# Hybrid RWKV-7 / Mamba-2 / short-convolution layer: two activation parts streamed side by side

## Chip, core and metric

The kernel runs on one core of a Trainium2 chip. The metric is device time in microseconds of that core for one execution, the median of three timed runs.

## What is computed

All data is fp32. One layer is applied to x of 256 tokens by 2048 channels:

```python
h = rmsnorm(x, norm_w[l])
p = h @ w_in[l]                                   # 2048 x 17552
pa, pb, pc, pg = jnp.split(p, ...)
oa = rwkv7_branch(pa, ...)                        # each 256 x 1024
ob = mamba2_branch(pb, ...)
oc = short_conv_branch(pc, sc_conv_w[l])
o = jnp.stack([oa, ob, oc], axis=2)
yb = jnp.einsum('btnw,nwd->btnd', o, w_branch[l]) # three products 1024 x 2048
gates = jax.nn.sigmoid(pg.reshape(bsz, seq, N_BRANCH, D_MODEL))
merged = jnp.sum(gates * yb, axis=2)
x = x + merged @ w_out[l]                         # 2048 x 2048
return rmsnorm(x, final_norm_w)
```

Nearly all the arithmetic is in the four dense products. The branches are a token shift and a delta-rule recurrence (RWKV-7, done in blocks of 32 tokens), a chunked state-space scan (Mamba-2) and a short convolution.

## The kernel before

**Split products.** A dense product is not done in plain fp32. Weight and activation are each split into a high part rounded to fp32r and a low part that is the rest; three fp32r matmuls add up in one accumulation: high weight by high activation, high weight by low activation, low weight by high activation. The weight tile (128 x 128) is the stationary operand, the activation (128 channels x 256 tokens) streams. `hhi` and `hlo` hold the parts of h, later of `merged`; `ohi` and `olo` those of a branch's output.

**Chunks and strips.** Weights arrive in chunks of 512 rows by 256 columns (`raw`, four slots). ScalarE rounds a chunk to `whi` (`split_hi`), VectorE subtracts to get `wlo` (`split_lo`), and TensorE takes it in two halves t = 0, 1 of 128 columns, four triples each (`half_chunk`, `triple`). Both splits run two chunks ahead of TensorE (`AHEAD`). Four chunks make a strip of two finished tiles, 256 columns of 2048 rows. A tile lies in columns 0 to 255 of a PSUM bank; strips use banks 0 and 1 or 2 and 3 in the order `BANKS = (0, 2, 0, 0, 2)`, so that the fourth strip of an iteration takes the banks of the third.

**Stages.** (1) 28 chunks: low-rank columns, B and C of Mamba-2 with their convolutions, the first r, k, v, g. (2) The branch loop, eight iterations j of 20 chunks (12 in the last), each for 128 channels. An iteration is written out by hand in 40 slots, one for each half chunk; at fixed slots every engine gets its piece of the branch work. For the prediction these matter: at slot 0 ScalarE exponentiates the decays and evicts the strip of v and g (`shift_pair`: a copy to `pq` and a scaled copy to `qq` of each tile); at 1 VectorE forms k, b and r with the decays; at 4 TensorE transposes them; at 5 ScalarE copies the transposes (`vt`, `kdbd`); at 5 and 7 VectorE masks the scores; at 8 ScalarE evicts x and z, at 9 to 12 VectorE does the conv taps and a triangular solve in 15 steps; at 16 the second, at 24 the third strip is evicted, at 32 the next r and k. TensorE's chain u, w, y and the states goes from slot 19 to 31. (3) The gates: for each of three branches, eight strips of four gate chunks (banks 2, 3) and two chunks of w_branch (y, banks 0, 1); ScalarE takes the sigmoid of the gate out of PSUM, VectorE multiplies by y out of PSUM and adds to `merged` (`gated`). The last iteration of the loop runs the first two gate strips. (4) The output stage, where `merged` is stationary and w_out streams in 256 columns: L1432 to L1434, 768 matmuls. (5) The tail: row sums, root, scaling, store.

**Order.** Each engine runs its list in the order written and waits on semaphores. `tile_done` and `chunk_used` tell of a finished tile; `tile_out` counts evicted tiles, and TensorE waits for it before it takes a bank again; `lo_done` counts split chunks. `gy_ok` counts the products with y.

## Time and profile before

| | |
|---|---|
| three runs | 1282.39 us median (1281.48 to 1282.54) |
| span of the profiled execution | 1279.8 us |
| busy | TensorE 97%, weight load 92%, VectorE 64%, ScalarE 46%, GpSimd 5% |
| granted TensorE clock | 0.997 of full speed, mean |
| chain that ended last | TensorE 81%, VectorE 9%, issue 4%, ScalarE 3% |
| DMA | 194.91 MB, 152 GB/s |

The profiled execution is one run, 0.2% under the median of the timed ones. Busy time is the time in which an engine has an instruction in flight. Matmuls overlap in the pipe (each is 283 ns long), so their sum is more than the span, and what one costs is seen from the distance between the starts of two. The chain that ended last is followed back from the end, at each step to what released it.

### The profile page before, as it was taken

What the parts mean: (1) busy time and instruction counts of PE and PEld (TensorE: products, weight loads), DVE (VectorE), ACT (ScalarE), POOL (GpSimd) and SP (SyncE); (2) the same over time, 40 slices, a digit from 0 to 9 for tenths busy, and PEclk for the clock granted to TensorE, in tenths of its full rate; (3) what the DMA queues carried; (4) which work ended last, traced back from release to release, by engine and by line L of the source; (5) the groups of instructions that cost most, each with busy time, mean ns of one, the idle gap of its engine ahead of it and who ended that gap; (6) DMA issues with size and microseconds to landing.
All of it is one profiled execution on the core that took longest, in us unless ns stands there. A gap on an engine that the chain in (4) does not pass through costs nothing.

```text
span 1279.8 us, 27520 instructions
## 1 busy us (share of the span) xinstructions
PE 1244.8 (97%) x10118; PEld 1175.6 (92%) x10118; DVE 822.3 (64%) x1340; ACT 589.2 (46%) x893; POOL 62.5 (5%) x93
## 2 busy tenths in 40 slices
PE   6999999999999999999999999999999999999996
PEld 5998889899898998998989989999999999999996
DVE  4787759578486695784867956654555455555653
ACT  5555346255354462643534535444444444335443
POOL 2001000010010000100001003000000000000000
PEclk9999999999999999999999999999999999999998
DMA  5774544445345344553544445465555666557652
GB/s 163 193 198 117 138 114 123 127 121 155 105 131 135 103 128 120 141 146 95 145 118 115 104 146 175 156 197 181 182 178 171 191 190 188 181 179 250 211 183 96
DMA packets 298623, 194.91 MB, mean 152 GB/s; under 512 B 23799, under 2 KB 297424, under 8 KB 297936
## 3 DMA queue, kind: packets, MB, share of 16 engines
q1 hardware_dynamic: 298308, 193.72, 51.8%
q8 instruction: 30, 0.49, 0.2%
q10 hardware_dynamic: 268, 0.56, 0.1%
q14 instruction: 17, 0.14, 0.0%
HBM read 191.61 MB, written 2.10 MB: 151 GB/s over the span
## 4 chain that ended last, share of the span: by engine, by line
PE 81%; DVE 9%; issue 4%; ACT 3%; DMA 1%; DVEq 0%; SPq 0%; ACTq 0%
PE ps L1153 21%; PE ps L1154 20%; PE ps L1155 20%; DVE lots L888 3%; PE ps L1434 2%; PE ps L1432 2%; PE ps L1433 2%; DVE lots L891 2%; PE ps L1326 1%; ACT work L571 1%; DVE wlo L731 1%; PE ps L1348 1%; PE ps L1328 1%; PE ps L1315 1%; PE ps L1316 1%
## 5 line engine op out<-in xcount | busy, mean ns | idle before, releaser
L1153 PE MATMUL ps<-hhi,whi 128*128 128x256 f32 x2208 | 645.2, 292 | 6.9 <-ACT lots L439 5.7
L1154 PE MATMUL ps<-hlo,whi 128*128 128x256 f32 x2208 | 624.3, 283 | 0.0
L1155 PE MATMUL ps<-hhi,wlo 128*128 128x256 f32 x2208 | 624.3, 283 | 0.0
L731 DVE TENSOR_TENSOR wlo<-raw,whi 128x1024 fp32r<-128x1024 f32 (+1 forms) x356 | 431.9, 1227 | 245.3 <-ACT whi L431 243.8
L431 ACT ACTIVATE whi<-raw 128x1024 fp32r<-128x1024 f32 (+1 forms) x356 | 371.3, 1052 | 289.9 <-PE ps L1155 251.8
L1153 PEld LDWEIGHTS ps<-hhi,whi 128*128 128x128 f32 x2208 | 421.1, 191 | 25.4 <-issue 18.6
L1154 PEld LDWEIGHTS ps<-hlo,whi 128*128 128x128 f32 x2208 | 421.5, 191 | 1.2
L1155 PEld LDWEIGHTS ps<-hhi,wlo 128*128 128x128 f32 x2208 | 421.1, 191 | 0.3
L1153 PE MATMUL ps<-ohi,whi 128*128 128x256 f32 x384 | 109.5, 285 | 0.0
L1155 PE MATMUL ps<-ohi,wlo 128*128 128x256 f32 x384 | 108.7, 283 | 0.0
L1154 PE MATMUL ps<-olo,whi 128*128 128x256 f32 x384 | 108.7, 283 | 0.0
L1153 PEld LDWEIGHTS ps<-ohi,whi 128*128 128x128 f32 x384 | 73.7, 192 | 0.1
L1154 PEld LDWEIGHTS ps<-olo,whi 128*128 128x128 f32 x384 | 73.7, 192 | 0.1
L1155 PEld LDWEIGHTS ps<-ohi,wlo 128*128 128x128 f32 x384 | 73.7, 192 | 0.0
L1432 PE MATMUL ps<-whi,hhi 128*128 128x256 f32 x256 | 72.5, 283 | 0.0
L1433 PE MATMUL ps<-wlo,hhi 128*128 128x256 f32 x256 | 72.5, 283 | 0.0
L1434 PE MATMUL ps<-whi,hlo 128*128 128x256 f32 x256 | 72.5, 283 | 0.0
L959 DVE TENSOR_TENSOR st<-ps,gcs 64x128 f32<-64x128 f32 x56 | 16.5, 295 | 51.9 <-PE ps L1348 51.4
L1432 PEld LDWEIGHTS ps<-whi,hhi 128*128 128x128 f32 x256 | 49.2, 192 | 0.0
L1434 PEld LDWEIGHTS ps<-whi,hlo 128*128 128x128 f32 x256 | 49.2, 192 | 0.0
L1433 PEld LDWEIGHTS ps<-wlo,hhi 128*128 128x128 f32 x256 | 49.2, 192 | 0.0
L888 DVE TENSOR_TENSOR lots<-lots 32x1 f32<-32x1 f32 (+14 forms) x120 | 35.0, 292 | 2.7
(251 smaller groups left out, 1150.3 us busy)
## 6 DMA issues: line engine op xcount, KB each, us to landing
raw<-in_w_in SPq DMA_DIRECT2D x548, 256.0 KB, 3.1
raw<-in_w_branch SPq DMA_DIRECT2D x96, 256.0 KB, 2.9
raw<-in_w_out SPq DMA_DIRECT2D x64, 256.0 KB, 2.9
o<-in_x SPq DMA_DIRECT2D x4, 1024.0 KB, 7.4
out_y<-lots SPq DMA_DIRECT2D x3, 512.0 KB, 5.1
lots<-in_final_norm_w SPq DMA_DIRECT2D x1, 1024.0 KB, 11.2
lots<-ad SPq DMA_DIRECT2D x32, 8.0 KB
tc<-lots SPq DMA_DIRECT2D x32, 8.0 KB
```

Of the source, the lines that this page charges most:

```text
L431: sc.activation(whi[:, slot, :, 0:width], raw[:, slot, :, 0:width], ACT.Copy).then_inc(hi_done, 1)
L571: op = sc.activation(kdbd[r, :, :, c, :], dkb[r, :, :, :], ACT.Copy)
L731: tt(wlo[:, slot, :, 0:width], raw[:, slot, :, 0:width], whi[:, slot, :, 0:width].bitcast(F32), ALU.subtract).then_inc(lo_done, 1)
L888: tt(prod, sol_n[:, r, a].unsqueeze(1).broadcast_to([32, k, k]), sol_t[:, a, a].rearrange("p i t -> p t i"), ALU.mult).then_inc(s["sol_p"], 1)
L891: v.tensor_reduce(sol_t[:, r, a], prod, AX.X, ALU.add).then_inc(s["sol_r"], 1)
L959: tt(st[64:128, :, c + 1, :], A[64:128, 0:128].rearrange("p (e n) -> p e n", e=2), gcs[64:128, :, c:c + 1].broadcast_to([64, 2, 64]), ALU. ...
L1153: mm(dst, a, khi, start=first, stop=False)
L1154: mm(dst, a, klo, start=False, stop=False)
L1155: return mm(dst, b, khi, start=False, stop=last)
L1432: mm(dst, hhi[:, kt, r], whi[:, q, k, :], start=kt == 0, stop=False)
L1433: mm(dst, hhi[:, kt, r], wlo[:, q, k, :], start=False, stop=False)
L1434: op = mm(dst, hlo[:, kt, r], whi[:, q, k, :], start=False, stop=kt == KT - 1)
```

## The change

- **Activation parts side by side.** `hx` holds high and low part of a channel tile next to each other (2 x 256 columns), `ox` those of a branch output; `hhi`, `hlo`, `ohi`, `olo` are views of them. `triple` becomes `product`: one matmul of `wlo` with the high part (256 columns), and one of `whi` with both parts (512 columns). The bank then holds high x high plus low x high in columns 0 to 255 and high x low in columns 256 to 511.
- **Halves added at eviction.** ScalarE copies columns 256 to 511 (`part_out`), and VectorE adds columns 0 to 255 to that (`fold`), which now counts `tile_out`. The scaled copy to `qq` (`mixed`), the tanh of z and of the short convolution's gate (`z_th`, `c_th`) and the sigmoids (`sg_ok`) read the folded tile from SBUF and wait for it. In `gated` both halves of y are multiplied by the gate and added: three operations for a tile where the first branch had one, four where the others had two.
- **Output stage in 512 columns.** Weights of w_out come in chunks of 256 rows by 512 columns; there are 384 matmuls of 512 columns, and evictions, squares and products with the final norm are 512 wide. The loops over strips are written out.
- Eight semaphores of the time-step computation become one (`dt_v`), with the same waits.

```diff
-            def triple(dst, wcol, slot, k, khi, klo, first, last):
-
-                a, b = whi[:, slot, k, wcol], wlo[:, slot, k, wcol]
-                mm(dst, a, khi, start=first, stop=False)
-                mm(dst, a, klo, start=False, stop=False)
-                return mm(dst, b, khi, start=False, stop=last)
+            def product(dst, wcol, slot, k, x, first, last):
+
+
+                mm(dst[:, 0:T], wlo[:, slot, k, wcol], x[:, 0, :], start=first, stop=False, skip_group_check=True)
+                return mm(dst, whi[:, slot, k, wcol], x.rearrange("p e t -> p (e t)"), start=False, stop=last,
+                          skip_group_check=True)
...
-                return sc.activation(dst, ps[:, bank, 0:T], ACT.Copy)
...
+            def proj(strip, t, bank, dst):
+
+                trailing(strip, t)
+                sc.activation(dst, ps[:, bank, T:2 * T], ACT.Copy).then_inc(part_out, 1)
+
+            def shift_pair(j, a, bank, strip, tiles):
+
+                for t in range(2):
+                    proj(strip, t, bank + t, pq[:, 2 * a + t, 1:1 + T])
                 for t in range(2):
                     w = 2 * a + t
-                    proj(strip, t, bank + t, pq[:, w, 1:1 + T])
-                    sc.activation(qq[:, w, :], ps[:, bank + t, 0:T], ACT.Copy,
-                                  scale=omm[:, bass.ds(j + w * CT, 1)]).then_inc(tile_out, 1)
+                    act.wait_ge(tile_out, tiles + t)
+                    sc.activation(qq[:, w, :], pq[:, w, 1:1 + T], ACT.Copy,
+                                  scale=omm[:, bass.ds(j + w * CT, 1)]).then_inc(mixed, 1)
...
+            def fold(n, bank, dst, rows=P):
+
+                dve.wait_ge(part_out, n + 1)
+                tt(dst, ps[0:rows, bank, 0:T], dst, ALU.add).then_inc(tile_out, 1)
...
                     if not first:
-                        act.wait_ge(s["gy_ok"], g - 1)
-                    sc.activation(sgt[:, t, :], ps[:, 2 + t, 0:T], ACT.Sigmoid).then_inc(tile_out, 1)
+                        act.wait_ge(s["y_out"], g - 1)
+                    sc.activation(sgt[:, t, :], ps[:, 2 + t, T:2 * T], ACT.Copy).then_inc(part_out, 1)
+                for t in range(2):
+                    act.wait_ge(tile_out, 16 * n + i * 4 + (MAIN_TILES + 2 * h + t + 1))
+                    sc.activation(sgt[:, t, :], sgt[:, t, :], ACT.Sigmoid).then_inc(s["sg_ok"], 1)
...
-                    gate, y_, gy_ = sgt[:, t:t + 1, :], ps[:, t:t + 1, 0:T], gy[:, t:t + 1, :]
-                    if n == 0:
-                        tt(m, gate, y_, ALU.mult).then_inc(s["gy_ok"], 1)
-                    else:
-                        tt(gy_, gate, y_, ALU.mult).then_inc(s["gy_ok"], 1)
-                        dve.wait_ge(s["gy_ok"], g + 1)
-                        tt(m, m, gy_, ALU.add).then_inc(s["mg_ok"], 1)
+                    gate, gy_, gz_ = sgt[:, t:t + 1, :], gy[:, t:t + 1, :], gz[:, t:t + 1, :]
+                    tt(m if n == 0 else gy_, gate, ps[:, t:t + 1, 0:T], ALU.mult).then_inc(s["gy_ok"], 1)
+                    tt(gz_, gate, ps[:, t:t + 1, T:2 * T], ALU.mult).then_inc(s["y_out"], 1)
+                    dve.wait_ge(s["gy_ok"], g + 1)
+                    if n > 0:
+                        tt(m, m, gy_, ALU.add).then_inc(s["mg_y"], 1)
+                        dve.wait_ge(s["mg_y"], g - 15)
+                    dve.wait_ge(s["y_out"], g + 1)
+                    tt(m, m, gz_, ALU.add).then_inc(s["mg_ok"], 1)
...
+            def outs(i):
+                for y in range(8):
+                    pe.wait_ge(lo_done, GATE_END + 1 + i * 8 + y)
...
+                        for k in range(2):
+                            kt = 2 * y + k
+                            r = slice(b * P, b * P + P)
+                            dst = ps[:, OUT_BANK[i] + b, :]
+                            mm(dst, hhi[:, kt, r], whi_o[:, y % RING, k, :], start=kt == 0, stop=False)
+                            mm(dst, hhi[:, kt, r], wlo_o[:, y % RING, k, :], start=False, stop=False)
+                            op = mm(dst, hlo[:, kt, r], whi_o[:, y % RING, k, :], start=False, stop=kt == KT - 1)
```

On ScalarE at slot 0 of an iteration, between the exponential of `lp` (lots) and the copies of the transposes, this stood (pq and lots<-ps,omm are the two copies of a tile out of PSUM, whi a split):

```order
L548 ACTIVATE lots<-lots 128x256 [waits cum_prev]
L436 REGISTER_ALU
L439 ACTIVATE pq<-ps 128x256 [waits tile_done]
L446 ISA
L446 ACTIVATE lots<-ps,omm 128x256
L438 ISA
L439 ACTIVATE pq<-ps 128x256 [waits chunk_used]
L446 ISA
L446 ACTIVATE lots<-ps,omm 128x256
L430 REGISTER_ALU [waits raw_in3]
L431 ACTIVATE whi<-raw 128x1024 [waits chunk_used]
```

In the changed kernel, at the same place:

```order
L533 ACTIVATE lots<-lots 128x256 [waits cum_prev]
L411 REGISTER_ALU
L418 ACTIVATE pq<-ps 128x256 [waits tile_done]
L413 ISA
L418 ACTIVATE pq<-ps 128x256 [waits chunk_used]
L426 ISA
L427 ISA [waits tile_out]
L427 ACTIVATE lots<-pq,omm 128x256
L426 REGISTER_ALU
L427 ISA [waits tile_out]
L427 ACTIVATE lots<-pq,omm 128x256
```

Both copies to `pq` come first, and the scaled copies read `pq` and wait for VectorE's `tile_out`; the splits stand behind that wait.

On VectorE, behind the products with the decays at slot 1 and ahead of the next splits, the changed kernel has the two folds and, for the shift, a wait for ScalarE's scaled copy:

```order
L923 SCALAR_TENSOR_TENSOR lots<-lots 128x256 [waits bv_ok]
L715 ISA
L716 TENSOR_TENSOR pq<-ps,pq 128x256 [waits part_out]
L715 REGISTER_ALU
L716 TENSOR_TENSOR pq<-ps,pq 128x256 [waits part_out]
L797 ISA
L798 ISA [waits mixed]
L798 SCALAR_TENSOR_TENSOR lots<-pq,prm,lots 128x256
L709 REGISTER_ALU
L710 TENSOR_TENSOR wlo<-raw,whi 128x1024 [waits hi_done]
```

Before, the shift followed the products at once. Two more folds stand at slot 9 ahead of the conv taps:

```order
L710 TENSOR_TENSOR wlo<-raw,whi 128x1024 [waits hi_done]
L715 REGISTER_ALU
L716 TENSOR_TENSOR xp<-ps,xp 128x256 [waits part_out]
L715 REGISTER_ALU
L716 TENSOR_TENSOR lots<-ps,lots 128x256 [waits part_out]
L725 ISA [waits tile_out]
L725 TENSOR_SCALAR lots<-xp,prm 128x256
```

There too the split and the conv tap were neighbours before.

## Rows read from the trace of the kernel before

**Rows 1.** The page, part 1: busy us, share of the span, instructions.

```profile
PE 1244.8 (97%) x10118; PEld 1175.6 (92%) x10118; DVE 822.3 (64%) x1340; ACT 589.2 (46%) x893; POOL 62.5 (5%) x93
```

**Rows 2.** Busy time by stretch: length, engines, granted clock, DMA share, GB/s.

```profile
374.20:458.75 84.55, 82.92 (x666) 74.62 (x668) 60.98 (x116) 39.92 (x69) 5.30 (x6) 1.00 0.46 126
...
765.00:1177.00 412.00, 412.00 (x3426) 410.94 (x3425) 222.43 (x246) 178.36 (x207) 10.00 (x9) 1.00 0.59 187
1177.00:1270.00 93.00, 92.75 (x773) 92.55 (x772) 52.07 (x68) 41.27 (x64) 0.00 (x0) 1.00 0.47 154
```

**Rows 3.** Timeline, TensorE in the gates: start us, duration us, instruction.

```profile
1000.07 0.28 PE L1154 MATMUL ps<-olo,whi 128*128 128x256 f32 x1
...
1003.91 0.28 PE L1153 MATMUL ps<-ohi,whi 128*128 128x256 f32 x1
```

**Rows 4.** Who waited for whom, TensorE: us in total, times, longest.

```profile
PE ps L1153 <- ACT lots L439: 5.7, 7, 0.8
...
PE ps L1153 <- DVE wlo L731: 1.2, 7, 0.2
```

**Rows 5.** Timeline with 16-wide weights; groups of weight loads there (busy, mean ns).

```profile
28.84 0.28 PE L1154 MATMUL ps<-hlo,whi 128*16 128x256 f32 x1
...
29.86 0.28 PE L1154 MATMUL ps<-hlo,whi 128*16 128x256 f32 x1
...
L1154 PEld LDWEIGHTS ps<-hlo,whi 128*128 128x128 f32 x19 | 3.6, 190 | 0.0
...
L1154 PEld LDWEIGHTS ps<-hlo,whi 128*16 128x16 f32 x16 | 1.5, 94 | 0.3
```

**Rows 6.** Chain that ended last, around 355 us: start, length, plain fp32, 256 columns.

```profile
355.32 0.43 PE ps L1205 x2
355.75 0.43 PE ps L1206 x2
```

**Rows 7.** Timeline in the first stage: VectorE's splits after the convolutions, TensorE's use.

```profile
62.13 3.50 DVE L731 TENSOR_TENSOR wlo<-raw,whi 128x1024 fp32r<-128x1024 f32 x3 [0.60 <-ACT whi L431]
...
64.76 0.28 PE L1153 MATMUL ps<-hhi,whi 128*128 128x256 f32 x1
```

**Rows 8.** Groups in the gates: busy us, mean ns, idle before and releaser.

```profile
L731 DVE TENSOR_TENSOR wlo<-raw,whi 128x1024 fp32r<-128x1024 f32 x141 | 171.4, 1232 | 130.6 <-ACT whi L431 130.4
...
L851 DVE TENSOR_TENSOR lots<-lots,ps 128x256 f32<-128x256 f32 x30 | 12.6, 421 | 32.2 <-PE ps L1155 32.2
```

**Rows 9.** Timeline, ScalarE, slots 0 to 6 of an iteration.

```profile
367.78 2.02 ACT L431 ACTIVATE whi<-raw 128x1024 fp32r<-128x1024 f32 x2
...
371.27 0.38 ACT L563 ACTIVATE lots<-ps 128x256 f32<-128x256 f32 x1 [0.70 <-PE ps L1271]
...
371.81 2.38 ACT L571 ACTIVATE work<-ps 32x512 f32<-32x512 f32 x4
374.21 2.01 ACT L431 ACTIVATE whi<-raw 128x1024 fp32r<-128x1024 f32 x2
```

**Rows 10.** Timeline, VectorE, slot 1: last product with the decays, then the shift.

```profile
368.33 0.42 DVE L923 SCALAR_TENSOR_TENSOR lots<-lots 128x256 f32<-128x256 f32 x1
368.67 0.48 DVE L806 SCALAR_TENSOR_TENSOR lots<-pq,prm,lots 128x256 f32<-128x256 f32 x1
```

**Rows 11.** Timeline, VectorE and TensorE at slot 18.

```profile
394.63 2.35 DVE L731 TENSOR_TENSOR wlo<-raw,whi 128x1024 fp32r<-128x1024 f32 x2
...
395.91 0.39 PE L1153 MATMUL ps<-hhi,whi 128*128 128x256 f32 x1 [0.17 <-DVE wlo L731]
```

**Rows 12.** Timeline, ScalarE and TensorE at slot 24.

```profile
415.54 0.66 ACT L439 ACTIVATE lots<-ps 128x256 f32<-128x256 f32 x2
...
416.05 0.38 PE L1153 MATMUL ps<-hhi,whi 128*128 128x256 f32 x1 [0.81 <-ACT lots L439]
```

**Rows 13.** VectorE at slots 17, 21 (timeline); TensorE at slot 19 (chain that ended last).

```profile
397.57 0.68 DVE L941 TENSOR_TENSOR lots<-tc,m16i 128x512 f32<-128x512 f32 x1
...
402.30 0.69 DVE L947 TENSOR_TENSOR lots<-ps,lots 128x512 f32<-128x512 f32 x1 [0.39 <-PE ps L1300]
...
399.04 0.89 PE ps L1293 x8
```

More of the change, by code:

```diff
@@ L746, in conv4, with fold_pair @@
                     conv_tap(done, at, ch, k)
+            def fold_pair(a, n, bank):
+                for t in range(2):
+                    fold(n + t, bank + t, pq[:, 2 * a + t, 1:1 + T])
             for k in range(KT):
@@ L769, in _ @@
                         m = 2 * (c // 4 - 2) + t
+                        fold(2 + m, 2 * ((c // 4) % 2) + t, xp[:, 3:3 + T])
                         dve.wait_ge(tile_out, 3 + m)
@@ L906, in main @@
                             gated(0, 0, 0)
+                    if t >= 2 * nchunks and t % 2 == 1 and (t // 2 - nchunks) % GATES == 4:
+                        gate_fold(0, 0, (t // 2 - nchunks) // GATES)
                     if t == 0:
@@ L981, in main @@
                     if t == 9:
+                        fold(nt, BANKS[0], xp[:, 3:3 + T])
+                        fold(nt + 1, BANKS[0] + 1, zp[:, 0, :])
                         dve.wait_ge(tile_out, nt + 1)
@@ L1019, in main @@
                             ).then_inc(s["ob_ok"], 1)
+                    if t == 32 and not last:
+                        fold_pair(0, nt + 6, BANKS[3])
                     if t == 33:
@@ L1439, in _ @@
-            outs(0, True)
-            with pe.Fori(1, 4) as i:
-                outs(i, False)
+            def outs(i):
+                for y in range(8):
+                    pe.wait_ge(lo_done, GATE_END + 1 + i * 8 + y)
+                    if i == 0 and y % 2 == 0:
+                        pe.wait_ge(s["m_lo"], y // 2 + 1)
+                    for b in range(2):
+                        if y == 0:
+                            if i == 0:
+                                pe.wait_ge(tile_out, MAIN_TILES + 48)
+                            elif i == 1:
+                                pe.wait_ge(s["y_out"], 48)
+                            else:
+                                pe.wait_ge(s["out_ok"], i * 2 + (b - 3))
+                        for k in range(2):
+                            kt = 2 * y + k
+                            r = slice(b * P, b * P + P)
[3 more added lines that the diff above has]
+                            op = mm(dst, hlo[:, kt, r], whi_o[:, y % RING, k, :], start=False, stop=kt == KT - 1)
+                        if y == 7 and b == 0:
+                            op.then_inc(s["out_mm"], 1)
+                    op.then_inc(chunk_used, 1)
@@ L1444 @@
+            for i in range(4):
+                outs(i)
 NAMES = ["x", "norm_w", "w_in", "rw_mu", "rw_w0", "rw_w2", "rw_a0", "rw_a2", "rw_kk", "rw_ka", "rw_rk", "rw_ln_w",
```

217 lines of the change are left out of this document (104 added, 113 removed).

## Prediction

> **What bounds the kernel now.** I read the page first: TensorE is busy 97% of the span, VectorE 64%, ScalarE 46% [rows 1]. A busy TensorE need not be at its peak, so the busy time by stage comes next [rows 2]: in the branch loop, 84.55 us for each of its iterations, TensorE shows 82.9 us; in the gates (412 us) and the output stage (93 us) it has no idle time, at the full granted clock (1.00, the 2.4 GHz level). What one matmul costs there is read from the starts. Between the two rows of [rows 3] lie 32 steps in 3.84 us: one 256-column matmul starts every 120 ns, while its 256 columns are 106.7 ns of a 2.4 GHz clock. So 13.3 ns of each, 11%, is not columns. Last, TensorE's waits [rows 4]: for eviction 5.7 us in all, for VectorE's splits 1.2 us. Short as they are, they are a warning: at one place of each iteration (slot 18, chunk 9) TensorE already starts within 0.2 us of the split it waits for. There VectorE, not TensorE, is late.
>
> **Products: three starts become two.** Before: 2592 triples of 256-column matmuls, 360 ns each. After: a 256-column and a 512-column one, 768 columns as before. The 256-column one is followed by a 128-wide weight load beneath it, just as now: 120 ns. No row shows 512 columns of fp32r, so I bound it. With a weight tile 16 wide the same 256-column matmul starts every 113.3 ns (9 steps in 1.02 us), and its load takes 94 ns, not 190 [rows 5]: so 6.7 of the 13.3 ns follow the size of the load and 6.7 remain when it is small. A plain fp32 pass that streams for 213 ns starts every 215 ns (0.43 us for two) with a 128-wide load beneath it [rows 6]: a stream that long hides the load. That puts a 512-column matmul between 215 and 213.3 + 6.7 = 220 ns; with the whole 13.3 ns fixed it is 227, with the excess growing by the column 240. I take 219, nearest to the long stream's row. The gain is 360 - 120 - 219 = 21 ns for a triple. By stage:
> - First 28 chunks (8 triples each): 224 x 21 ns = 4.7 us. VectorE's slack after a pair of convolutions is 64.76 - 63.3 = 1.4 us (the first of three splits from 62.13 ends about 63.3) [rows 7]; two folds with their hand-overs take 1.0 and the faster TensorE 0.5, so a tenth is lost in each of four strips: -4.4 us.
> - Gates: 144 chunks, 1152 x 21 ns = -24.2 us. Per strip of six chunks VectorE gains two folds and four more operations on gate and y, six at 0.42 us, 2.5 us; its splits wait for ScalarE 130.6 us over this stage [rows 8], 5.4 us per strip. ScalarE's copies and the late sigmoids must free banks 2 and 3 within the two y chunks, 5.4 us: one split by ScalarE 1.06, two copies 0.8, two folds 0.8 are done after some 3 us. Nothing here reaches TensorE; without that cover each strip would pay the fold pair, 0.8 us.
> - Output: 768 matmuls of 240 ns per pair become 384 of 219: -8.1 us. The same bytes arrive, in longer rows. The tail behind the last matmul gets three 512-wide operations on VectorE where 256-wide ones stood, 0.69 against 0.42 us [rows 8, 13]: +0.8 us.
>
> **The branch loop: what the folds cost.** A tile is now evicted by ScalarE (upper half) and then VectorE (add the lower half). Ten folds an iteration, 0.42 us each, about 0.34 in a row. Three pairs matter.
> - Slots 0/1 (pq for v and g). The fold stands on VectorE behind the products of k and b, which end at 368.7 [rows 10]. ScalarE, which finished its four reads of PSUM and went on to two splits at 367.78 [rows 9], now waits for that fold before its scaled copies. Reckoned through: fold to 369.1, copy to 369.5, second copy to 369.85, two splits to 371.85, two acm copies to 372.7, where the copies behind the transposes began at 371.27. It had 0.70 us of idle time before them, so 1.4 us is lost net. Behind it stand, in ScalarE's order, vt, four kdbd copies (371.81 to 374.2) and the split at 374.21, and on that one VectorE's whole solve. That is the chain that ended last here: +1.4 us.
> - Slot 9 (xp, z): two folds ahead of the conv taps and the solve, in the same full stretch of VectorE, which ends with the split from 394.63 that TensorE takes at 395.91 with no slack [rows 11]: +0.7 us.
> - Slot 24: strips 2 and 3 use the same banks, so TensorE already waits 0.81 us for the copy of the first tile [rows 12]; the fold follows that copy: +0.45 us.
> The other two pairs (slots 16, 32) fall beside TensorE work: slot 16 pushes tdt (ready about 398.25) to about 398.95 against a use at 399.04 [rows 13], 0.15 us lost against a faster TensorE; slot 32 has VectorE idle before it. Against these: TensorE is the bound from slot 20 to slot 35, about 68 triples x 21 ns = 1.4 us gained; from there to slot 4 VectorE is full and the gain is idle time. Sum: 2.1 + 0.45 + 0.15 - 1.4 = +1.3 us an iteration, +11 us for eight (the last has only the first half, with little to gain).
>
> **Sum.** -4.4 + 11 - 24.2 - 8.1 + 0.8 = -24.9 us. Against the profiled 1279.8 us that is 1254.9; the median of the runs shown lies 2.6 us above that execution's span, so the forecast is 1257.5, say 1257 us.
>
> **Rivals.**
> 1. The whole 13.3 ns is a price of each instruction (512 columns cost 227). For it: nothing in the trace separates load and start above 6.7 ns in fp32r. Against: 215 ns for the long fp32 stream. Saving 13.3 ns: -2.7 and -15.3 and -5.1 us; the loop loses 2.7 - 0.9 = 1.8 us an iteration, +14; tail +0.8. Together -8: 1274 us.
> 2. Both streams run free: 111 ns (eight fp32 128-wide passes start in 0.89 us [rows 13]) and 215 ns. Saving 34 ns: -6 - 39 - 9.6 us, loop +0.4 x 8 = +3, tail +0.8, together -51: 1231 us. Against it: every 256-column fp32r start with a 128-wide load beneath shows 120.
> 3. The slower side: the excess belongs to the columns, and only the 1.7 ns over 213.3 that the fp32 pass shows is fixed. Then a triple saves 1.7 ns: -0.3 - 2 - 0.7 us, while the loop pays 2.7 - 0.1 = 2.6 us eight times, +21, tail +0.8, together +19: 1301 us. Where a triple saves under about 10 ns, the folds win. For it: 240 is simply twice 120. Against it: the 16-wide rows. The Trainium skill's page "TensorE: Matmul & The Clock Gate", section "Back-to-back issue gap", speaks for this one: a warm matmul of N columns takes N/2.4 + 2.5 ns, 109 for 256 and 216 for 512, so cutting the same columns otherwise would save only 2.5 ns a triple, and its time would be near this rival's. The trace's 120 ns is not its 109.
> 4. The folds are dearer than reckoned: all five hand-overs of a pair are exposed, at 1.4 us each as at slot 1, 7 us an iteration instead of 2.7, +35 us more: 1292 us. It decides from about 3 us more an iteration. Against it: idle VectorE before slots 24 and 32.
>
> **How the numbers follow.** Chances: forecast 0.52, rival 1 0.20, rival 2 0.07, rival 3 0.08, rival 4 0.07, something between 4 or 3 and no change 0.06. The forecast's own bounds: 215 or 220 ns for 512 columns (-6 or +1 us), +0.5 to +2.3 us an iteration (-6 or +8): 1245 to 1268. The range must reach over rival 1 with the loop 6 us dearer, 1280; below it stops at 1244, leaving out most of rivals 2, 3 and 4, 0.2 in all. A measurement of this kernel can tell about 0.2% from no change, 1279.8 to 1285. Faster 0.82, same 0.03, slower 0.15.
>
> **What would show it.** In the gates of the changed kernel, starts 120 and 219 ns apart in turn (227: rival 1; 111 and 215: rival 2; 238: rival 3), so the strips of the gates at 16.3 us, not 17.3. In the loop, ScalarE's scaled copies of pq at slot 0 idle some 1.5 us for VectorE's fold, iterations of 85.8 us, more than before, and more TensorE waits for VectorE's split at slot 18. In the output stage 384 matmuls in about 84 us. An iteration shorter than 84.5 us would prove the fold chain wrong; one over 88 us would be rival 4.

## The result: 7 us slower, not 25 us faster

The changed kernel takes 1289.12 us (median of 4 runs, 1287.53 to 1290.0), the kernel before 1282.05 us (4 runs, 1281.48 to 1282.54): a ratio of 1.0054, with 1.004 to 1.0068 as its 95% interval. The forecast was 1257 us, the range 1244 to 1280. The profiled executions are 1287.9 us (after) and 1279.8 us (before) long.

The page of the changed kernel, part 1 (engine, busy us and share, instructions), against [rows 1]:

```profile
PE 1224.8 (95%) x7142; PEld 1012.8 (79%) x7142; DVE 899.9 (70%) x1558; ACT 606.2 (47%) x925; POOL 62.7 (5%) x93
```

TensorE has 2976 matmuls fewer and 20 us less busy time, VectorE 78 us more, and the span is 8 us longer: the time went into waits. Busy time by stretch says where. Each stretch below begins and ends at the start of a stage's first product (columns: length, then busy us and instructions of PE, PEld, DVE, ACT and POOL, granted clock, DMA share, GB/s). First the kernel before, gates and output stage:

```profile
753.40:1177.44 424.04, 424.04 (x3538) 422.12 (x3538) 229.44 (x258) 182.98 (x215) 10.73 (x10) 1.00 0.58 184
1177.44:1269.72 92.28, 92.28 (x770) 92.11 (x768) 51.42 (x66) 40.83 (x64) 0.00 (x0) 1.00 0.47 154
```

Then the changed kernel: the whole loop, one iteration of it, the gates, their last strip, the output stage.

```profile
107.14:771.77 664.63, 631.09 (x3837) 501.30 (x3835) 492.97 (x972) 309.96 (x525) 40.39 (x45) 0.99 0.46 123
...
282.06:368.86 86.80, 82.15 (x505) 65.32 (x504) 64.17 (x127) 40.28 (x68) 5.32 (x6) 1.00 0.46 122
...
771.77:1188.85 417.08, 412.50 (x2386) 359.80 (x2385) 277.65 (x400) 200.13 (x262) 10.79 (x10) 1.00 0.60 187
...
1168.32:1188.85 20.53, 17.13 (x98) 14.64 (x96) 10.92 (x15) 8.99 (x12) 0.00 (x0) 1.00 0.83 299
1188.85:1277.06 88.21, 87.64 (x384) 71.90 (x384) 50.34 (x54) 38.34 (x48) 0.00 (x0) 1.00 0.52 161
```

Set against the forecast, in us, from the starts of the first product of each stage:

| stage | before | after | change | forecast |
|---|---|---|---|---|
| first 28 chunks | 88.79 | 89.42 | +0.6 | -4.4 |
| branch loop | 646.54 | 664.63 | +18.1 | +11 |
| gates | 424.04 | 417.08 | -7.0 | -24.2 |
| output stage | 92.28 | 88.21 | -4.1 | -8.1 |
| tail | 10.1 | 10.8 | +0.8 | +0.8 |

A full iteration has gone from 84.53 to 86.80 us; the first one of the changed kernel takes 88.12 us, 1.3 more than the six behind it, and the last, which has 12 chunks, 0.9 us more than before. TensorE's waits in the changed kernel (who waited for whom: us in total, times, longest), against [rows 4]:

```profile
PE ps L1247 <- DVE ad L875: 15.2, 8, 1.9
...
PE ps L1156 <- DVE lots L716: 8.9, 7, 1.3
...
PE ps L1156 <- DVE wlo L710: 4.4, 13, 1.1
PE ps L1430 <- issue: 3.4, 1, 3.4
```

L1247 is `score(1)` of slot 6, which waited for nothing worth a line before; L716 is the fold of slot 24, which took the place of ScalarE's copy (0.8 us a time before, now 1.3); L1430 is the first matmul of the output stage.

**The price of a product.** Two strips of the gates, of 48 products each, as first matmul of a strip and first of the next (start us, duration us):

```profile
916.60 0.28 PE L1156 MATMUL ps<-hx,wlo 128*128 128x256 f32 x1
916.71 0.39 PE L1157 MATMUL ps<-hx,whi 128*128 128x512 f32 x1
916.94 0.28 PE L1156 MATMUL ps<-hx,wlo 128*128 128x256 f32 x1
...
933.24 0.28 PE L1156 MATMUL ps<-hx,wlo 128*128 128x256 f32 x1
```

```profile
1100.48 0.28 PE L1156 MATMUL ps<-hx,wlo 128*128 128x256 f32 x1
...
1117.44 0.28 PE L1156 MATMUL ps<-hx,wlo 128*128 128x256 f32 x1
```

The first strip is 16.64 us, 346.7 ns a product: 13.3 ns less than the 360 of before, and 26.7 ns more than its 768 columns take at 2.4 GHz, so 13.3 ns for each of the two matmuls on average. That is rival 1's number for a product, not the 339 ns of the forecast. The split between the two is not rival 1's: over 430 products from 920 to 1070 us the next start lies 117 ns behind a 256-column matmul and 230 ns behind a 512-column one, not 120 and 227. The second strip is 16.96 us, 353.3 ns a product (117 and 236 ns): the same code, at the same granted clock of 1.00, has a second, slower spacing that lasts for whole stretches (here from strip 16 on, the third branch; the first stage has it too, from the wait at 63.95 us to 87 us). No row of the kernel before showed anything like it.

**Where the loop waits.** The changed kernel at slots 1 to 6 (start us, duration us, instruction, in brackets the idle time ahead and what ended it):

```profile
375.69 0.42 DVE L923 SCALAR_TENSOR_TENSOR lots<-lots 128x256 f32<-128x256 f32 x1
376.03 0.74 DVE L716 TENSOR_TENSOR pq<-ps,pq 128x256 f32<-128x256 f32 x2
...
376.58 0.91 ACT L427 ACTIVATE lots<-pq,omm 128x256 f32<-128x256 f32 x2 [2.05 <-DVE pq L716]
...
377.40 1.99 ACT L406 ACTIVATE whi<-raw 128x1024 fp32r<-128x1024 f32 x2
...
378.47 2.36 DVE L710 TENSOR_TENSOR wlo<-raw,whi 128x1024 fp32r<-128x1024 f32 x2 [0.74 <-ACT whi L406]
...
380.75 0.28 DVE L872 TENSOR_TENSOR adt<-ps,m16s 128x128 f32<-128x128 f32 x1
...
383.33 0.71 PE L1247 MATMUL ps<-lots 64*128 64x256 f32 x4 [1.91 <-DVE ad L875]
```

In the kernel before the same score operation on VectorE stands at:

```profile
371.33 0.28 DVE L874 TENSOR_TENSOR adt<-ps,m16s 128x128 f32<-128x128 f32 x1
```

Before, it begins 3.00 us behind the start of the last product with the decays (368.33, [rows 10]); after, 5.06 us behind it. The chain is the one that the prediction named: products, folds, scaled copies, splits by ScalarE, splits by VectorE, and each hand-over is there to be seen. It costs 2.06 us here, not 1.4.

### The profile page after: what moved, and what is told of

It reads as the page before. It is cut to its first block, busy times and chain, and to the rows that moved or that the text cites. A ratio compares the mean times of both kernels' runs of the same rounds, so it can differ in the third digit from the quotient of the medians.

```text
span 1287.9 us, 21850 instructions
## 1 busy us (share of the span) xinstructions
PE 1224.8 (95%) x7142; PEld 1012.8 (79%) x7142; DVE 899.9 (70%) x1558; ACT 606.2 (47%) x925; POOL 62.7 (5%) x93
## 4 chain that ended last, share of the span: by engine, by line
PE 61%; DVE 23%; issue 7%; ACT 6%; DMA 1%; DVEq 1%; ACTq 0%; SPq 0%; POOL 0%
PE ps L1157 28%; PE ps L1156 16%; DVE wlo L710 6%; ACT whi L406 3%; DVE lots L886 3%; PE ps L1430 2%; PE ps L1432 2%; PE ps L1431 2%; DVE lots L889 2%; PE ps L1328 1%; PE ps L1350 1%; PE ps L1330 1%; ACT work L556 1%; DVE lots L1044 1%; DVE lots L723 1%
## 5 line engine op out<-in xcount | busy, mean ns | idle before, releaser
L1157 PE MATMUL ps<-hx,whi 128*128 128x512 f32 x2208 | 783.6, 395 | 0.0
L1156 PE MATMUL ps<-hx,wlo 128*128 128x256 f32 x2208 | 644.3, 292 | 13.7 <-DVE lots L716 8.9
L1157 PEld LDWEIGHTS ps<-hx,whi 128*128 128x128 f32 x2208 | 415.2, 188 | 88.5
L1156 PEld LDWEIGHTS ps<-hx,wlo 128*128 128x128 f32 x2208 | 417.4, 189 | 37.4 <-issue 20.2
L1157 PE MATMUL ps<-ox,whi 128*128 128x512 f32 x384 | 135.3, 394 | 0.0
L1156 PE MATMUL ps<-ox,wlo 128*128 128x256 f32 x384 | 108.6, 283 | 0.0
L1157 PEld LDWEIGHTS ps<-ox,whi 128*128 128x128 f32 x384 | 72.1, 188 | 16.4
L1156 PEld LDWEIGHTS ps<-ox,wlo 128*128 128x128 f32 x384 | 72.6, 189 | 0.1
L1430 PE MATMUL ps<-whi,hx 128*128 128x512 f32 x128 | 50.0, 391 | 4.0 <-issue 3.4
L1431 PE MATMUL ps<-wlo,hx 128*128 128x512 f32 x128 | 49.9, 389 | 0.0
L1432 PE MATMUL ps<-whi,hx 128*128 128x512 f32 x128 | 49.8, 389 | 0.0
L716 DVE TENSOR_TENSOR lots<-ps,lots 128x256 f32<-128x256 f32 (+1 forms) x89 | 35.6, 419 | 11.8 <-ACT lots L500 11.8
L1430 PEld LDWEIGHTS ps<-whi,hx 128*128 128x128 f32 x128 | 24.0, 188 | 9.6 <-issue 3.7
```

The lines of the kernel that those rows point to most:

```text
L716: tt(dst, ps[0:rows, bank, 0:T], dst, ALU.add).then_inc(tile_out, 1)
L1156: mm(dst[:, 0:T], wlo[:, slot, k, wcol], x[:, 0, :], start=first, stop=False, skip_group_check=True)
L1157: return mm(dst, whi[:, slot, k, wcol], x.rearrange("p e t -> p (e t)"), start=False, stop=last, skip_group_check=True)
L1430: mm(dst, hhi[:, kt, r], whi_o[:, y % RING, k, :], start=kt == 0, stop=False)
L1431: mm(dst, hhi[:, kt, r], wlo_o[:, y % RING, k, :], start=False, stop=False)
L1432: op = mm(dst, hlo[:, kt, r], whi_o[:, y % RING, k, :], start=False, stop=kt == KT - 1)
```

## Experiments

**1. The output stage alone** (`outs_only`): the kernel before with its output stage in 512 columns, everything else as it was.

```diff
-                                 mm(dst, hhi[:, kt, r], whi[:, q, k, :], start=kt == 0, stop=False)
+                            mm(dst, hhi[:, kt, r], whi_o[:, y % RING, k, :], start=kt == 0, stop=False)
```

> The kernel before with the output stage alone in 512 columns (384 matmuls of 512 columns, w_out in rows of 512, three 512-wide operations behind the last). Theory A, a fixed price of some 13.3 ns for each matmul: 384 x 13.3 = 5.1 us less TensorE time, of which the changed kernel showed 4.2 in this stage (92.04 to 87.82 us), against a tail 0.9 us longer: 1278.5 to 1279 us (-3.3 us), and no stall ahead of the first output matmul, as there is none before. Theory B, the 3.8 us stall ahead of the output stage in the changed kernel comes with the output stage itself (its first weights land later): the same stall is here, and the time is 1282 us, no gain. Theory C, folds and products of the other stages made even this part what it was: nothing here differs from 1282 by more than 0.5 us.

Measured: 1277.11 us (6 runs), a ratio of 0.9965 (0.9952 to 0.9977), 4.6 us faster than before: theory A, a little better than expected. The stage and two starts with 30 steps between them:

```profile
1176.93:1264.27 87.34, 87.33 (x384) 72.01 (x384) 49.20 (x50) 38.44 (x48) 0.00 (x0) 1.00 0.53 166
```

```profile
1199.50 0.39 PE L1426 MATMUL ps<-whi,hhi 128*128 128x512 f32 x1
...
1206.30 0.39 PE L1426 MATMUL ps<-whi,hhi 128*128 128x512 f32 x1
```

6.80 us for 30 steps are 226.7 ns a matmul of 512 columns, 213.3 of them columns. The last strip ahead of the stage is 0.2 us longer than the others here (17.49 us), so the changed kernel's stall of 3.4 us does not come from the output stage's longer rows.

**2. Gates and output stage, without the loop and the first stage** (`gates_outs2`). The products of the first 28 chunks and of the loop stay `triple`, their evictions ScalarE's alone; `half_chunk` has a second form for the gates. The time-step computation counts on one semaphore, as in the changed kernel. (An earlier form of this kernel, `gates_outs`, gave no time, so nothing rests on it.)

```diff
-                    half_chunk(c, (base + y) % RING, q, t, 2)
+                    wide_chunk(c, (base + y) % RING, q, t, 2)
```

> The kernel before with the gates and the output stage as changed; the first stage and the branch loop stay three 256-column matmuls with ScalarE's evictions (the small dt chain of the first stage shares one counter, as in the changed kernel). Theory A, the losses are the loop's and the first stage's, the gains of the gates and the output stay: first stage 88.8 and loop 646.6 us as before; gates 414.5 us where all 24 strips take the 16.64 us of the quick spacing, 420 where they take the 16.96 us of the slow one (424.0 before); output 88.2 (87.3 with the output stage changed alone): 1277.1 - 4.2 to 9.7 + 0.9, so 1268 to 1274 us. Theory B, the loop is slower for the layout of the activations side by side (kept here: high and low parts interleaved by tile) and not for the folds: iterations over 85.5 us and a time of 1276 or more.

Measured: 1270.38 us (4 runs, 1269.04 to 1275.61), ratio 0.9924 (0.9902 to 0.9946). The first stage is 88.79 us and the loop 646.64 us, as before: the layout costs nothing (theory B falls), the folds of those two stages cost all. The gates are 414.3 us. Ten strips, the last strip, and the first 5.3 us of the output stage:

```profile
914.44:1080.85 166.41, 166.41 (x961) 146.51 (x960) 110.58 (x163) 79.17 (x102) 0.00 (x0) 1.00 0.61 190
1147.41:1167.70 20.29, 16.80 (x98) 14.47 (x96) 10.89 (x15) 8.98 (x12) 0.00 (x0) 0.99 0.83 304
1167.70:1173.00 5.30, 5.30 (x17) 4.25 (x18) 5.23 (x11) 1.48 (x3) 0.00 (x0) 0.70 0.36 100
```

The ten strips are all of 16.64 us. The last one has the stall, and something came with it: the granted clock is 0.70 in the stretch behind. The output stage's first matmuls:

```profile
1167.70 0.76 PE L1462 MATMUL ps<-whi,hx 128*128 128x512 f32 x1 [3.49 <-DVE hx L1073]
1168.26 0.63 PE L1463 MATMUL ps<-wlo,hx 128*128 128x512 f32 x1
...
1170.39 0.61 PE L1462 MATMUL ps<-whi,hx 128*128 128x512 f32 x1
```

From the second on they start every 427 ns (2.13 us for 5 steps), which is 512 columns at 1.2 GHz, until TensorE is back at 227. Six such steps and the first one of 0.56 us are 1.5 us more there. The stage as a whole keeps 0.6 of it: from its first to its last start it takes 88.4 us, against 87.8 in the changed kernel, whose clock did not fall.

**3. The stall ahead of the output stage** (`gates_outs_tail`): the same kernel with the eviction of the last strip's gate tiles ahead of the split that waits for the first w_out transfer.

```diff
+                            early = tail and h == 1 and q == 4
+                            if early:
+                                sigmoids(n, i, h)
                             gate_split(n, i, h * GATES + q + AHEAD)
-                            if q == 4:
+                            if q == 4 and not early:
                                 sigmoids(n, i, h)
```

and `gate_fold` and `gate_split` on VectorE in the same way.

> The kernel gates_outs2 with one more edit: in the last strip of the gates ScalarE's two copies and sigmoids stand ahead of the split that waits for the first w_out transfer, and VectorE's two folds ahead of its split of that chunk. Theory A, the stall ahead of the first output matmul (the last strip takes 19.4 to 20.5 us in the kernels with changed gates, against 17.5 with the output stage alone changed) is the chain copies - folds - sigmoids behind that transfer: the last strip falls under 18 us, and the time by 2 to 3.5 us against gates_outs2, to 1265 to 1271. Theory B, it is the transfer of the first w_out chunk itself that is late: the last strip stays over 19 us and the time is that of gates_outs2 within 0.5 us.

Measured: 1267.01 us (4 runs, 1266.1 to 1271.55), ratio 0.9882 (0.9865 to 0.9898): the fastest of all kernels here, 15 us under the kernel before. The last strip, and the first output matmul:

```profile
1153.42:1170.81 17.39, 17.13 (x97) 14.62 (x96) 11.00 (x15) 9.26 (x12) 0.00 (x0) 1.00 0.90 332
```

```profile
1170.81 0.47 PE L1468 MATMUL ps<-whi,hx 128*128 128x512 f32 x1 [0.26 <-issue]
```

The stall was 3.49 us and is 0.26. Theory A holds. The wait for the transfer alone is not enough: in `outs_only`, where the sigmoid stands alone behind a wait of 5.36 us, the last strip is 0.2 us longer. This is the chain in the changed kernel, copies, folds and sigmoids, behind that one wait of ScalarE:

```profile
1181.97 1.06 ACT L406 ACTIVATE whi<-raw 128x1024 fp32r<-128x1024 f32 x1 [6.67 <-DMA raw<-in_w_out]
...
1184.20 0.75 DVE L716 TENSOR_TENSOR lots<-ps,lots 128x256 f32<-128x256 f32 x2
...
1184.65 0.75 ACT L503 ACTIVATE lots<-lots 128x256 f32<-128x256 f32 x2 [1.08 <-DVE lots L716]
...
1186.25 2.94 ACT L628 ACTIVATE hx<-work 128x1024 fp32r<-128x1024 f32 x3
...
1188.84 0.48 PE L1430 MATMUL ps<-whi,hx 128*128 128x512 f32 x1 [3.40 <-issue]
```

The medians of experiments 2 and 3 are 3.4 us apart, but their profiles are 1269.04 and 1271.55 us: the profile of `gates_outs_tail` fell into the slow spacing from strip 5 on (18 strips of 16.96 us, +5.8 us), the one of `gates_outs2` nowhere.

**4. Three starts again** (`three_starts`): the 512-column matmul of a gate product as two of 256, into both halves of the same bank, everything else as in `gates_outs2`.

```diff
-                    op = mm(dst, whi[:, slot, k, wcol], x[:, kt, :, :].rearrange("p e t -> p (e t)"), start=False,
-                            stop=kt == nq * KC - 1, skip_group_check=True)
+                    for e in range(2):
+                        op = mm(dst[:, e * T:e * T + T], whi[:, slot, k, wcol], x[:, kt, e, :],
+                                start=False, stop=kt == nq * KC - 1, skip_group_check=True)
```

> The kernel gates_outs2 with the 512-column matmul of each gate product written as two of 256 columns, into the lower and the upper half of the same bank: the columns, weights, folds and banks are those of gates_outs2, only the starts are three again. Theory A, a fixed price for each matmul: a product takes 360 ns again, strips 17.28 us, the gates 1152 x 13.3 ns = 15.3 us longer than in gates_outs2's quick spacing (8 us longer than in the slow one), and the time 1282 to 1285 us: the folds without the gain, with the stalls at strip 4 and ahead of the output stage partly hidden again. Theory B, the price goes by columns or by bank halves: a product stays at 347 to 353 ns and the time at that of gates_outs2.

Measured: 1282.90 us (10 runs), ratio 1.0004 (0.9994 to 1.0013). One strip, from its first start to the next strip's:

```profile
970.55 0.28 PE L1195 MATMUL ps<-hx,wlo 128*128 128x256 f32 x1
...
987.83 0.28 PE L1195 MATMUL ps<-hx,wlo 128*128 128x256 f32 x1
```

17.28 us, 360 ns a product, the strip of the kernel before to the hundredth, with folds, layout and banks of the changed one. So a third matmul for the same columns costs 13.3 ns, and no strip shows the slow spacing. The third start has a weight load of its own, so this run can't tell the price of a start from that of a load.

**5. The loop without its folds** (`loop_no_fold`): the changed kernel, ScalarE copying the lower half and nobody reading the upper one.

```diff
-                sc.activation(dst, ps[:, bank, T:2 * T], ACT.Copy).then_inc(part_out, 1)
+                sc.activation(dst, ps[:, bank, 0:T], ACT.Copy).then_inc(tile_out, 1)
...
-                        fold_pair(1, nt - 2, BANKS[4])
```

(and the four other pairs of folds in `main` likewise).

> The changed kernel with the ten folds of each loop iteration left out: ScalarE copies the lower half of the bank and gives the bank free itself, and the upper half (weight's high part x activation's low part) is never read, so the outputs lack that product. The products stay a 256- and a 512-column matmul. Theory A, the folds and the chain through VectorE are the loop's whole loss: iterations fall from 86.8 to 84.55 less what TensorE gains where it is the bound, 68 x 13.3 ns = 0.9 us, so 83.6 us, and the time to 1289 - 7.6 x 3.2 = 1265 us (1263 to 1268). Theory B, the loss is in TensorE's own starts (the slower spacing, 353 ns a pair): iterations stay over 85.5 us and the time over 1279.

Measured: 1270.46 us (4 runs, 1265.18 to 1271.03), ratio 0.9901 (0.9877 to 0.9925). An iteration:

```profile
276.15:359.91 83.76, 81.49 (x505) 65.28 (x504) 60.94 (x117) 40.16 (x68) 5.32 (x6) 1.00 0.47 127
```

83.76 us, as theory A had it (83.6). So the ten folds cost 86.81 - 83.76 = 3.05 us an iteration, and two starts a product instead of three bring 84.53 - 83.76 = 0.77 us. Even free folds would gain only 0.8 us here. The time is 5 us over the expectation. Most of that is the gates' slow spacing: 18 strips of 16.96 us in this profile, 5.8 us, where the changed kernel's profile has 2.4.

**6. One pair of folds left out at a time** (`no_fold_slot1`, `no_fold_slot9`, `no_fold_slot24`), the edit of experiment 5 for that pair alone.

> The changed kernel with the fold pair of slot 1 (tiles v and g) left out in every iteration: ScalarE copies the lower bank halves and frees the banks; the upper half of these two tiles isn't read, so their high x low product is missing. Iterations are 86.81 us with all ten folds and 83.76 with none. Theory A, the chain at slots 0 to 4 is the main cost: VectorE's first score operation came 2.06 us later behind the products of slot 1 than in the kernel before, so the iteration falls by about 2.0, to 84.8 us, and TensorE's 1.9 us wait ahead of score(1) is gone. My sum had 1.4 here: 85.4. Theory B, VectorE is simply full until the solve and each pair costs its own 0.7 us: 86.1.

> The changed kernel with the fold pair of slot 9 (tiles xp and z) left out in every iteration, in the same way. My sum had 0.7 us an iteration for it, as it stands in VectorE's full stretch ahead of the solve: 86.1 us. Rival: the conv taps and the solve wait for other things there by now (PE's score(1) comes 2 us later), so that it costs under 0.3 us: 86.5 or more.

> The changed kernel with the fold pair of slot 24 (scb tiles) left out in every iteration, in the same way. TensorE waits 1.3 us for this fold, 0.8 us for ScalarE's copy in the kernel before. My sum had 0.45 us: 86.35 us. Rival: the stretch behind is bound by TensorE's and VectorE's chain through the states of slots 24 to 31 and not by this wait, so nothing is gained: 86.8.

One execution each, at 1273.7, 1283.11 and 1284.41 us, so the iterations must decide; those of one execution repeat to some hundredths, but for two of slot 9's. For slot 1, and for slot 9 (two iterations):

```profile
278.66:363.79 85.13, 82.08 (x505) 65.31 (x504) 63.33 (x125) 40.26 (x68) 5.32 (x6) 1.00 0.46 125
```

```profile
281.11:367.15 86.04, 81.94 (x505) 65.33 (x504) 63.52 (x125) 40.28 (x68) 5.32 (x6) 1.00 0.46 123
367.15:453.45 86.30, 82.92 (x505) 66.57 (x504) 63.62 (x125) 40.27 (x68) 5.33 (x6) 0.98 0.46 123
```

Against 86.81 us: slot 1 gives back 1.68 us (my sum had 1.4, theory A 2.0), slot 9 gives 0.77 (0.7), slot 24 gives 0.58 (iterations of 86.23; 0.45). For slot 9 that is by the iterations at a granted clock of 1.00; the two at 0.98 give back 0.5. Together 3.03 of the 3.05 us: the costs add, and by subtraction slots 16 and 32 cost next to nothing (neither was left out by itself). Without slot 1's pair VectorE's first score operation is again 3.00 us behind the products in every iteration, so the whole 2.06 us of that chain hang on this pair; 1.68 of them reach the iteration.

**7. The scaled copies behind a split** (`late_mix`).

```diff
                         shift_pair(j, 1, BANKS[4], strip0 - 1, nt - 1)
+                    if t == 3:
+                        mix_pair(j, 1, nt - 1)
```

> The changed kernel with one thing moved: in the loop ScalarE's two scaled copies of the pair pq for v and g, which wait for VectorE's fold, stand behind the split of slot 2 instead of ahead of it, and VectorE's shift of v behind its split of slot 2. Theory A, the chain products - fold - scaled copies - splits at slots 0 to 4 makes the 1.9 us wait of TensorE ahead of score(1) in slot 6: that wait shrinks to under 1 us, VectorE's first score operation comes 1.0 to 1.3 us sooner behind the products of slot 1, TensorE may wait 0.5 us for the shift, and the time falls by 4 to 8 us, to 1281 to 1285. Theory B, VectorE's work up to the solve is what is full, and the order on ScalarE only says where the wait shows: the iterations stay 86.8 us, and the time 1288 to 1290.

Measured: 1282.32 us (10 runs, 1280.77 to 1286.38), ratio 1.001 to the kernel before (1.0 to 1.0019), 6.8 us under the changed kernel; iterations of 85.89 us. VectorE's first score operation and TensorE's `score(1)`:

```profile
376.83 0.28 DVE L879 TENSOR_TENSOR adt<-ps,m16s 128x128 f32<-128x128 f32 x1
...
379.42 0.71 PE L1255 MATMUL ps<-lots 64*128 64x256 f32 x4 [0.43 <-DVE ad L882]
```

The last product began at 372.90, so the score comes 3.93 us behind it (5.06 before the edit, 3.00 in the kernel before), and the wait of 1.91 us is 0.43. Theory A: 1.13 of the chain's 2.06 us were ScalarE's order; the other 0.93 stay as long as the folds do (with them left out, experiment 6, all 2.06 are gone). The iteration gains 0.92 us, although TensorE now waits 0.5 us in it for the shift.

**8. A fold sooner in the first stage** (`first_fold`).

```diff
                     v.reciprocal(dts[:, 5, :], dts[:, 3, :]).then_inc(s["dt_v"], 1)
+                    fold_pair(0, PRE_TILES - 4, 0)
...
-                    fold_pair(0, PRE_TILES - 4, 0)
```

> The changed kernel with one line moved: the fold pair of the first stage's tiles r and k stands on VectorE right behind the reciprocal of the time-step chain, not behind the whole chain and the four products with the causal mask. Theory A: in the changed kernel ScalarE's scaled copies wait 5.56 us for this fold, its three splits and VectorE's shift of k come 2.5 us later than in the kernel before (104.07 against 101.55 us), and TensorE waits 1 us at chunk 26 and some 0.3 us more ahead of the loop; with the fold 4 us sooner these waits go, the shift comes 1.2 us sooner, and the first stage takes 88.0 to 88.4 us instead of 89.4 (88.8 in the kernel before); the loop and the rest stay. The time falls by 1.0 to 1.4 us, which the changed kernel's own spread hides in part: 1286.5 to 1289. Theory B: the first stage ends with the chain through the masks and the time steps, which this edit makes 0.7 us longer, and the stage stays at 89.4 us or more.

The stage in this kernel:

```profile
18.00:106.09 88.09, 87.20 (x507) 73.79 (x507) 69.71 (x112) 45.76 (x72) 2.60 (x2) 1.00 0.67 177
```

88.09 us instead of 89.42, as theory A had it. What it repairs, in the changed kernel:

```profile
98.77 0.51 ACT L427 ACTIVATE lots<-pq,omm 128x256 f32<-128x256 f32 x1 [5.56 <-DVE pq L716]
...
101.94 0.39 PE L1156 MATMUL ps<-hx,wlo 128*128 128x256 f32 x1 [0.83 <-DVE wlo L710]
```

But the whole took 1292.87 us (4 runs, 1287.06 to 1295.01), more than the changed kernel, not less. The profile of this kernel (span 1291.8 us) has the gates at 420.0 us (all strips from 5 on in the slow spacing, +2.9 us) and the output stage at 90.2 us (+2.0: 13 matmuls every 427 ns behind a stall of 2.8 us). Neither stage was edited, but that the moved line has no part in them is not shown; the expectation for the total was too sure.

**9. The slow spacing.** Two orders of the gates' matmuls: in `hi_first` the 512-column one of a product comes first; in `grouped` (on `gates_outs_tail`) the four of 256 columns of half a chunk come first, then the four of 512.

```diff
                 for k in range(KC):
                     kt = q * KC + k
                     mm(dst[:, 0:T], wlo[:, slot, k, wcol], x[:, kt, 0, :], start=kt == 0, stop=False,
                        skip_group_check=True)
+                for k in range(KC):
+                    kt = q * KC + k
                     op = mm(dst, whi[:, slot, k, wcol], x[:, kt, :, :].rearrange("p e t -> p (e t)"), start=False,
```

> The kernel gates_outs2 with the two matmuls of a product in the other order in the gates: 512 columns of whi first, then 256 of wlo. Theory A, a price of some 13 ns for each matmul whatever its length: a pair again takes 346.7 ns, strips 16.64 us. On the slower spacing (353.3 ns a pair, 3 pairs in 1.060 us): if it comes from the 256-column matmul that starts a bank's lower half just ahead of the 512-column one, it is gone here, all strips 16.64 us and the gates 414.5 us or less; if it belongs to the alternation of the two lengths as such, it shows here too, in whole stretches, 16.96 us a strip, and the time lies in 1268 to 1274 us as for gates_outs2.

> The kernel gates_outs_tail with the gates' eight matmuls of half a chunk in another order: first the four of 256 columns (wlo), then the four of 512 (whi), instead of the two lengths in turn. Theory A, a fixed price for each matmul: 4 x 120 + 4 x 226.7 = 1386.7 ns, the same as four pairs of 346.7; and if the slower spacing (353.3 ns a pair) comes from the two lengths in turn, it is gone: every strip 16.64 us, the times of its executions within 2 us of each other, 1264.5 to 1267 us. Theory B, the slower spacing belongs to the 512-column matmuls wherever they stand: strips of 16.96 us show here too in some stretches, and the times spread over 5 us as those of gates_outs_tail do (1266.1 to 1271.6). Theory C, a change of length costs something itself (116 + 230 ns are both unlike 120 and 227): then a half chunk differs from 1386.7 ns by more than 5.

`hi_first`: 1273.72 us (4 runs), ratio 0.9931 (0.9914 to 0.9947); strips of 16.96 us from strip 3 to strip 22 but for strip 4. So the slow spacing does not hang on which of the two comes first, and its excess lies behind the 512-column one again (117 and 237 ns). `grouped`: 1270.27 us (5 runs, 1269.91 to 1270.79), ratio 0.9912 (0.9898 to 0.9925):

```profile
1000.86 0.64 PE L1202 MATMUL ps<-hx,wlo 128*128 128x256 f32 x4
1001.34 1.09 PE L1206 MATMUL ps<-hx,whi 128*128 128x512 f32 x4
1002.27 0.63 PE L1202 MATMUL ps<-hx,wlo 128*128 128x256 f32 x4
```

Four of 256 columns in 0.48 us, four of 512 in 0.93: 232 ns each where the output stage shows 227, and 16.84 us for nearly every strip. Half a chunk takes 1403 ns, not 1387 (against A), in every stretch alike (against B's stretches). It is more than 5 ns off, which was theory C's sign, but C's reason fails: this order changes length a quarter as often as the products in turn, whose quick spacing has no excess over 1387. The excess sits in the 512-column matmuls. The executions of this kernel lie within 0.9 us of each other, those of `gates_outs_tail` within 5.5: an order that never takes the quick spacing is steadier and slower. What decides which spacing a stretch takes stays open.

## Why the prediction was wrong, step by step

- **"I take 219, nearest to the long stream's row": the step that failed first.** 512 columns cost 226.7 ns in the output stage, and a product of 256 and 512 columns takes 346.7 ns, as 120 + 226.7 would give (the starts lie 117 and 230 ns apart). The value came from a row of another kind, a plain fp32 pass of 213 ns [rows 6], which was near in length and not in type. The 16-wide rows [rows 5] showed that the load's size matters, not that a long stream hides it. A triple saves 13.3 ns instead of 21, shown by experiments 1 and 4: 8.8 us less in the gates (1152 x 7.7 ns), 3 us in the output stage, 1.7 us in the first. The Trainium skill's page "TensorE: Matmul & The Clock Gate", section "Back-to-back issue gap", would give 216 ns for 512 columns and 109 for 256; the traces show 226.7 and 120, and their difference to the columns is the same 13.3 ns at both lengths: columns plus a constant fits here, a constant of 2.5 ns does not. The section calls the rule the gap of a single isolated matmul, with no room in it for a weight load, and for a stream of loads and matmuls it gives about 131 ns at 512 columns; the 226.7 ns measured here, in fp32r, are far from that too.
- **The loop's mechanism was right, its sum short.** The forecast had 1.4 + 0.7 + 0.45 + 0.15 us of cost and 1.4 of gain, +1.3 us an iteration. Measured: 1.68 + 0.77 + 0.58 + 0 = 3.03 and a gain of 0.77, +2.26, against 2.27 between the iterations. The gain fell with the price of a product (68 triples x 13.3 ns are 0.9). At slot 1 the term subtracted ScalarE's idle 0.70 us from 2.1; VectorE's score operation came the full 2.06 us later. The first iteration's 1.3 us more were not in the sum at all; their cause is not shown.
- **"VectorE's slack after a pair of convolutions is 1.4 us": right place, but not the only one.** From start to start TensorE loses 0.66 and 0.46 us at chunks 14 and 18, some tenths more than reckoned, and 1.0 us at chunk 26 that the step did not look for: the fold of r and k stands behind the whole time-step chain, and ScalarE's splits behind it (experiment 8: 1.3 us of the stage). Some 60 of the stage's 224 products are in the slow spacing besides, 0.4 us.
- **"Nothing here reaches TensorE" in the gates failed, above all at two of 24 strips.** The 5.4 us of VectorE's waits per strip [rows 8] were a mean. In the last strip ScalarE stands 6.67 us in a wait for a transfer with the evictions behind it (3.6 us over a strip of that spacing, experiment 3). In strip 4 the group norm fills VectorE:

```profile
854.18 4.63 DVE L710 TENSOR_TENSOR wlo<-raw,whi 128x1024 fp32r<-128x1024 f32 x4
```

```profile
855.46 0.39 PE L1156 MATMUL ps<-hx,wlo 128*128 128x256 f32 x1 [1.10 <-DVE wlo L710]
```

  The four splits stand late behind `gated`; the strip takes 18.02 us instead of 16.64 (17.28 before). That the group norm's operations delayed them is read from the trace, not tried. Strips 0 to 2 gain 0.9 us together, not the 1.9 that 13.3 ns a product would give; why is not traced.
- **Missed altogether: the slow spacing** (+2.4 us in the gates of this profile), which no row before could show, and the lower clock behind a stall, which cost this kernel's output stage nothing. The clock could not have been read from [rows 2], which has no such stall.
- **Right:** the tail (+0.8 us, measured 0.8); the sign and place of the chain at slots 0 to 4 with its 1.5 us of ScalarE's idle time (2.05 us at L427). That there is a price of a product below which the folds win was right too, but not its size: the forecast put it at about 10 ns, and at 13.3 they have won.
- **Rival 1** had the mechanism, and 1274 us. What came on top of its sum is the loop (+4), the first stage (+3), the gates' two strips and their spacing (+8), the output stage (+1). Its chance of 0.20 was too small, and the range had its upper end 9 us too low, since every loss of cover was priced as if only one thing could be late. The slower side was given to rival 3, whose mechanism did not occur, and to rival 4, which came only in part: three of its five hand-overs cost something, 3.03 us an iteration and not 7. Several small exposures together made the loss.

The gain was not a wrong idea: where TensorE is the bound it is there (gates and output stage: `gates_outs_tail` at 0.988). In the loop and the first stage VectorE was already due at the same instants, and a second evicting engine in the chain gave back more than TensorE won.

## To carry to other kernels

Price a longer matmul by a row of the same type and say what is fixed in it; a fixed 13 ns per instruction is worth having only where TensorE never waits. Split such a change by stage before judging it: it won 11 us in two stages (15 with the last strip repaired) and lost 19 in the two others. A mean of slack over a stage hides the one strip in which an engine stands in front of a transfer: look for the longest wait of the evicting engine and what is queued behind it.

## What the runs showed of the hardware

- In a stream of one length, with a 128-wide weight load for each matmul, an fp32r matmul of 256 columns starts every 120.0 ns (`before`) and one of 512 every 226.7 ns (`outs_only`) at full clock: columns plus 13.3 ns. At the lower level the steps are 427 ns for 512 columns (`gates_outs2`), which is the columns alone.
- Products of 256 and 512 columns in turn have two spacings, 346.7 and 353.3 ns (three products in 1.060 us), each held for strips on end, at a granted clock of 1.00; 117 ns lie behind the 256-column one in both, 230 or 236 behind the other. Changes were seen behind TensorE's waits at 63.95 us and at strip 4, and inside strip 16, the first of the third branch; what brings them is open. Three starts of 256 never showed it. Four executions of `gates_outs_tail` spread by 5 us, where 15 of the kernel before spread by 1.3; that the spacing makes the difference fits its one profile and is not shown for the others.
- Behind waits of 3.49 and 2.81 us ahead of the output stage the granted clock was at the 1.2 GHz level for 6 and 13 steps of 427 ns (`gates_outs2`, `first_fold`), while in the changed kernel it stayed at 1.00 behind one of 3.40 us, and in `late_mix` behind one of 2.97. So the wait's length alone does not decide it. The stage took 87.8 us from first to last start without such steps, 88.4 with 6 and 89.8 with 13. In the changed kernel's loop such a stretch cost next to nothing (iterations of 86.80 to 86.85 us with it, 86.80 and 86.81 without): this iteration has some 3 us of it, behind slot 6, and the length of its neighbour with none. In `no_fold_slot9` (experiment 6) the iterations that have it are 0.26 us longer.

```profile
195.26:282.06 86.80, 83.25 (x506) 66.54 (x505) 64.19 (x127) 40.28 (x68) 5.32 (x6) 0.98 0.45 122
```

```profile
210.00:215.00 5.00, 5.00 (x23) 4.09 (x21) 4.35 (x8) 3.13 (x5) 0.00 (x0) 0.66 0.66 171
```
